# First queries and keys of the prompt's latent attention loaded ahead of stores, and two more page groups of the sample stage fetched within that attention

## The reference

```python
def block(args):                      # mla_prompt, one block of 128 queries
    ql, qr, start = args
    s = (jnp.einsum('bqhc,bkc->bhqk', ql, ckv)
         + jnp.einsum('bqhr,bkr->bhqk', qr, krope)) * MLA_SCALE
    qpos = start + jnp.arange(Q_BLOCK)
    p, _ = masked_softmax_stats(s, kpos[None, :] <= qpos[:, None])
    return jnp.einsum('bhqk,bkc->bqhc', p.astype(ckv.dtype), ckv)
...
ckv_past = cache_ckv[l, page_table].reshape(Bd, past, KV_LORA)
kr_past = cache_krope[l, page_table].reshape(Bd, past, QK_ROPE)
o_lat = mla_sample(ql, qr, ckv, kr, ckv_past, kr_past)
k_cat = jnp.concatenate([cache_win_k[l], kb], axis=1)
```

## Time and profile before

| | before |
|---|---|
| median of three runs | 1953.33 us (1951.91 to 1961.49) |
| profiled execution | 1959.79 us, span 1958.1 us |
| TensorE busy | 1887.9 us, 96% of the span |
| VectorE, ScalarE, GpSimd busy | 1055.5, 887.8, 431.5 us |
| mean granted clock of TensorE | 0.990 |
| DMA | 270.80 MB, mean 138 GB/s |

### The profile page before, as it was taken

One profiled execution on the slowest core, in us unless ns is written; L12 is line 12 of the kernel. 1 busy time (PEld: TensorE's weight loads), 2 busy tenths in 40 slices (PEclk: granted clock), 3 DMA queues, 4 the chain that ended last, 5 costly groups with the idle time before them and its releaser, 6 DMA issues. The chain is left out here.

```text
span 1958.1 us, 47133 instructions
## 1 busy us (share of the span) xinstructions
PE 1887.9 (96%) x18076; PEld 1466.6 (75%) x18076; DVE 1055.5 (54%) x3034; ACT 887.8 (45%) x2042; POOL 431.5 (22%) x569
## 2 busy tenths in 40 slices
PE   7999999999999899999999799999999999999998
PEld 6989898876787667776677466666666688888886
DVE  4433333687854467767677455555556752232232
ACT  5222222688832345566556444344444553333332
POOL 0111111256002130133101322232222411111110
PEclk9999999999999899999999899999999999999999
DMA  8534343743466510112001599777884653333331
GB/s 300 157 108 118 103 122 94 216 124 122 136 167 178 162 55 21 45 44 61 26 18 53 169 297 240 238 217 229 234 247 146 213 194 107 97 97 108 118 101 51
DMA packets 192238, 270.80 MB, mean 138 GB/s; under 512 B 37176, under 2 KB 152328, under 8 KB 183128
## 3 DMA queue, kind: packets, MB, share of 16 engines
q1 hardware_dynamic: 172344, 170.27, 31.0%
q0 software_dynamic: 19712, 98.01, 14.6%
HBM read 212.99 MB, written 54.95 MB: 137 GB/s over the span
## 5 line engine op out<-in xcount | busy, mean ns | idle before, releaser
L102 PE MATMUL proj_acc<-proj_w_hi,proj_x_hi 128*128 128x512 f32 (+2 forms) x512 | 183.9, 359 | 10.2 <-DVE proj_x_lo L372 8.4
L104 PE MATMUL proj_acc<-proj_w_hi,proj_x_lo 128*128 128x512 f32 (+2 forms) x512 | 182.0, 356 | 0.0
L103 PE MATMUL proj_acc<-proj_w_lo,proj_x_hi 128*128 128x512 f32 (+2 forms) x512 | 182.0, 355 | 0.0
L1857 DVE CUSTOM_DVE_ANT_0 mla_probs<-mla_scores,keep_in_rms 128x512 f32<-128x512 f32 x192 | 124.8, 688 | 64.6 <-PE mla_scores L1731 64.2
L1807 ACT ACTIVATE mla_probs<-mla_probs,mla_bias 128x256 f32<-128x256 f32 (+15 forms) x128 | 153.0, 1196 | 12.0 <-DVE mla_bias L1861 7.2
L1731 PE MATMUL mla_scores<-prompt_kr_parts,mla_q_parts 64*128 64x512 f32 (+3 forms) x640 | 136.7, 373 | 0.0
L2208 PE MATMUL dec_scores<-dec_keysT,sample_q_lat 128*64 128x256 f32 x1024 | 124.0, 382 | 3.0 <-DVE dec_keysT L2387 1.8
L2318 ACT ACTIVATE dec_keysT<-dec_turned 128x512 f32<-128x512 f32 (+1 forms) x160 | 89.4, 560 | 65.4 <-PE dec_turned L2164 65.1
L2324 ACT ACTIVATE dec_pT<-dec_outs 128x256 f32<-128x256 f32 x80 | 30.8, 385 | 192.3 <-PE dec_outs L2230 157.8
L102 PEld LDWEIGHTS proj_acc<-proj_w_hi,proj_x_hi 128*128 128x128 f32 x512 | 97.4, 190 | 21.1 <-issue 8.4
L2208 PEld LDWEIGHTS dec_scores<-dec_keysT,sample_q_lat 128*64 128x64 f32 x1024 | 75.4, 138 | 41.2 <-ACT dec_probs L2338 5.0
(11 more groups left out here) (468 smaller groups left out, 4880.2 us busy)
## 6 DMA issues: line engine op xcount, KB each, us to landing
win_v_tile<-wv_out SPq DMA_DIRECT2D x75, 128.0 KB
memory_x_raw<-in_xT SPq DMA_DIRECT2D x17, 512.0 KB, 5.4
proj_rows<-in_x SPq DMA_DIRECT2D x17, 512.0 KB, 4.0
featT<-proj_featT POOLq DMA_DIRECT2D x34, 256.0 KB, 2.8
late_ckv<-in_xT SPq DMA_DIRECT2D x17, 512.0 KB, 6.7
late_ckv<-in_x SPq DMA_DIRECT2D x17, 512.0 KB, 4.3
y_out<-host_buf POOLq DMA_DIRECT2D x16, 512.0 KB, 6.5
dec_k_rows<-in_win_k SPq DMA_DIRECT2D x64, 96.0 KB
```

Source lines behind the costliest of these rows:

```text
L102: pe.matmul(out, lh, rh, start=start, stop=False)
L103: pe.matmul(out, lh, rl, start=False, stop=False)
L104: return pe.matmul(out, ll, rh, start=False, stop=stop)
L1857: dve.tensor_tensor_reduce(probs[:, u % 2, w, c * CH:c * CH + wide], scores[:, n % 3, 0:wide], add, -MLA_SCALE, -LOWEST, ALU.add, ALU.min, ...
```

## The change

Four things are changed.

1. In the latent projections SP issues `first.load` in chunk 2, behind that chunk's key store and the load of chunk 3's input and ahead of the stores of its queries. It stood in chunk 3 behind those stores. The keys of chunk 2 are no longer in it.
2. `first.load_third` stands behind the last key store as before, and now also loads the keys of chunk 2 and the queries of unit 3 (once GpSimd has split unit 1: `q_ready` 2), all ahead of the last stores of queries. `load_q(3)` is gone from the attention's own list.
3. ScalarE's cast of the keys of chunk 2 (`cast_third`) stands ahead of its last product and no longer ahead of five of them.
4. GpSimd fetches three groups of pages (`EARLY`) in the latent attention where it fetched one. Groups 1 and 2 go to `pages_ahead`, in the memory of the even heads' split keys, when the third pair of heads is scored. In the sample stage GpSimd clears the window parts first and then starts from group 3; slots 1 and 2 are empty at first, so that groups 6 and 7 need not wait for a slot. The window rows of sample 1 lie over `pages_ahead`, and their loads also wait for the values of groups 1 and 2.

```diff
-        self.page, self.page_kr = self.buf[:, 0:SEQ], self.buf[:, SEQ:SEQ + self.KR]
-        self.page_loaded, self.page_kr_loaded = b.sem("page_loaded"), b.sem("page_kr_loaded")
+        self.page = self.buf[:, 0:SEQ]
+        self.pages_kr = [self.buf[:, SEQ + l * self.KR:SEQ + (l + 1) * self.KR] for l in range(self.EARLY)]
+        self.pages_loaded, self.pages_kr_loaded = ([b.sem(f"{n}_loaded{l}") for l in range(self.EARLY)] for n in ("page", "page_kr"))
...
-                if c == NCK - 1:
-                    sp.wait_ge(ahead.shares_stored, 16)
-                    sp.wait_ge(new_valued, DEC_B // 2)
-                    sp.wait_ge(k_stored, 16 * c)
-                    sp.wait_ge(qn_stored, 16)
-                    sp.wait_ge(qr_stored, 64)
-                    first.load(sp)
                 sp.wait_ge(act_kept, kept_on_act(c, 7))
                 sp.wait_ge(dve_kept, kept_on_dve(c, 7))
                 sp.dma_start(io["mla_k"].rearrange("(g p) t -> p g t", p=P)[:, :, cols], k_nope[:]).then_inc(k_stored, 16)
                 if c + 1 < NCK:
                     load_cq(c + 1)
-                else:
-                    sp.wait_ge(qn_stored, 16 * c)
-                    sp.wait_ge(qr_stored, 64 * c)
+                if c == NCK - 2:
+                    sp.wait_ge(ahead.shares_stored, 16)
+                    sp.wait_ge(new_valued, DEC_B // 2)
+                    sp.wait_ge(k_stored, 32)
+                    sp.wait_ge(qn_stored, 16)
+                    sp.wait_ge(qr_stored, 64)
+                    first.load(sp)
+                if c == NCK - 1:
+                    sp.wait_ge(qn_stored, 32)
+                    sp.wait_ge(qr_stored, 128)
                     first.load_third(sp)
...
+                        if c == NCK - 1 and i == PER - 2:
+                            first.cast_third(act)
...
-        even_k_hi, even_k_lo = (b.sb(n, [P, SEQ], F32R) for n in ("even_k_hi", "even_k_lo"))
+        with ExitStack() as until_last_heads:
+            even = Buffers(nc, until_last_heads, "mla", owner=owner)
+            even_k_hi, even_k_lo = (even.sb(n, [P, SEQ], F32R) for n in ("even_k_hi", "even_k_lo"))
+        pages_ahead = b.sb("pages_ahead", [P, Host.EARLY - 1, SEQ])
...
-            sp.dma_start(k_raw[:, 2 * CH:3 * CH], io["mla_k"][0:P, 2 * CH:3 * CH]).then_inc(first_k_loaded[2], 16)

         def load_third(sp):
             sp.wait_ge(first_q_ready, 2)
             sp.dma_start(qn_raw[:, 0, :], io["mla_qn"][0:P, 2 * CW:3 * CW]).then_inc(q_loaded[0], 16)
             sp.dma_start(qr_raw[:, 0, :], io["mla_qr"][0:P, 2 * CW:3 * CW]).then_inc(q_loaded[0], 16)
+            sp.wait_ge(prompt.k_stored, 48)
+            sp.dma_start(k_raw[:, 2 * CH:3 * CH], io["mla_k"][0:P, 2 * CH:3 * CH]).then_inc(first_k_loaded[2], 16)
+            sp.wait_ge(q_ready, 2)
+            sp.dma_start(qn_raw[:, 1, :], io["mla_qn"][0:P, 3 * CW:4 * CW]).then_inc(q_loaded[1], 16)
+            sp.dma_start(qr_raw[:, 1, :], io["mla_qr"][0:P, 3 * CW:4 * CW]).then_inc(q_loaded[1], 16)

         def cast_first_k(act, c):
...
-            load_q(3)
...
-            rows = bass.IndirectOffsetOnAxis(ap=sample.rows_of[:, 0:1], axis=0)
+            rows = [bass.IndirectOffsetOnAxis(ap=sample.rows_of[:, l:l + 1], axis=0) for l in range(host.EARLY)]
             pool.wait_ge(k_ready, 4 * (H_A // 2 - 1))
-            pool.indirect_dma_start(host.page, None, ckv_rows, rows).then_inc(host.page_loaded, 16)
+            pool.indirect_dma_start(host.page, None, ckv_rows, rows[0]).then_inc(host.pages_loaded[0], 16)
+            pool.wait_ge(scores_done, 2 * unit_end[NI * (H_A // 2 - 1) - 1])
+            for l in range(1, host.EARLY):
+                pool.indirect_dma_start(pages_ahead[:, l - 1, :], None, ckv_rows, rows[l]).then_inc(host.pages_loaded[l], 16)
             pool.wait_ge(q_ready, 2 * (NU - 1))
-            pool.indirect_dma_start(host.page_kr, None, kr_rows, rows).then_inc(host.page_kr_loaded, 16)
+            for l in range(host.EARLY):
+                pool.indirect_dma_start(host.pages_kr[l], None, kr_rows, rows[l]).then_inc(host.pages_kr_loaded[l], 16)
...
+                if s == 1:
+                    sp.wait_ge(pv_done, past_item[1] + 1)
...
-        for n in range(1, NP):
-            if n == 2:
-                clear_window_parts()
+        clear_window_parts()
+        for n in range(EARLY, NP):
             u = n % AHEAD
-            if 2 <= n < AHEAD:
-                pool.wait_ge(k_turned, 4 * (past_item[n - 2] + 1))
-            if n >= AHEAD:
+            if n >= AHEAD + EARLY:
                 pool.wait_ge(kr_turned, n - AHEAD + 1)
             rows = bass.IndirectOffsetOnAxis(ap=rows_of[:, n:n + 1], axis=0)
             pool.indirect_dma_start(kr[:, u, :], None, kr_rows, rows).then_inc(kr_loaded[u], 16)
-            if n >= AHEAD:
+            if n == AHEAD or n >= AHEAD + EARLY:
                 pool.wait_ge(pv_done, past_item[n - AHEAD] + 1)
             pool.indirect_dma_start(slots[u].rearrange("p m c -> p (m c)"), None, ckv_rows, rows).then_inc(ckv_loaded[u], 16)

...
-                if l:
-                    pe.wait_ge(ckv_loaded[l % AHEAD], 16 * (l // AHEAD + (1 if l % AHEAD else 0)))
-                rows = slots[l % AHEAD]
+                if l >= EARLY:
+                    pe.wait_ge(ckv_loaded[l % AHEAD], loads_of(l))
+                else:
+                    pe.wait_ge(host.pages_loaded[l], 16)
+                rows = page_at(l)
```

48 lines of the change are left out of this document (28 added, 20 removed).

## The result

| | before | after |
|---|---|---|
| median of three runs, us | 1953.33 (1951.91 to 1961.49) | 1935.06 (1932.14 to 1936.93) |
| profiled execution, us (span) | 1959.79 (1958.1) | 1932.14 (1930.4) |
| mean granted clock | 0.990 | 0.995 |

The ratio is 0.9903, 95% interval 0.9877 to 0.9929: 18.3 us less between the medians, forecast 15.8. Two later measurements of the same two kernels gave 0.9916 (0.9896 to 0.9935) and 0.9918 (0.9900 to 0.9937), 16 us.

The account below looks back on a forecast made before the run. TensorE, busy for 96% of the span, was taken as the bound, with time to win at two seams. Latent start -10.5 and sample start -5.3 gave 1953.33 - 15.8 = 1937.5 us; range 1932 to 1947 us.

Parts of the forecast that it names:

- The loads ahead of the stores: Latent start: SP issues the first loads by 634 us, ahead of the query stores; VectorE free at 661.1, not 665.4.
- The 3.46 us stall: Latent start: TensorE's wait for VectorE at the second tile of a score step, to shrink to some 0.5 us.
- the 4.46 us one: Latent start: TensorE's wait ahead of 685.35 for GpSimd's split of unit 3's queries, to vanish with their earlier load.
- The chain of short waits: Latent attention's first score steps: six TensorE pauses of 0.6 us at full clock, 3.6 us; third turn done at 675.6.
- The last store is late next: Latent start: last query store lands at 678.2 and holds VectorE; the step from 689.26 begins at 679.5, 9.8 us earlier.
- Size of the latent half: Latent start: the whole gain there, -10.5 us, with bounds of -5 and -12.5.
- The clock rival: Latent attention's ramp: short pauses make TensorE's clock fall; gain there and at sample start only 13 us, 1940.5 us; chance 0.20.
- two waits of 1.67 and 1.66 us at the sample start that the clock survived: Sample start: argument against the clock falling, since it stood at 1.00 from 1110 to 1115 after such waits.
- The sample start: Sample stage's start: waits of 1.67, 1.66 and 1.96 us for groups 1 to 3 fall, -5.3 us; bounds nothing to -6.
- The rival that the fetch would not cure the wait ahead of group 3's turn: Sample start: that wait names "issue", not a DMA, so only 2 us are won there; 1941 us in all; chance 0.14.
- the copy behind the window mask: Sample start: VectorE's copy for group 1's values ends at 1116.6, and group 3's scores start at 1118.5, not 1123.87.
- The chances: Whole kernel: forecast keeps 0.48; faster 0.76, same 0.16, slower 0.08, with 1943.6 us as the border.

Follow-up runs that it names:

- experiment 5: Changed kernel, but unit 3's queries asked for behind the last query stores, as in the kernel before; ratio to the kernel before 0.9938.
- Experiment 7: Changed kernel with the last chunk's plain query store issued ahead of the four rotary stores; ratio to the kernel before 0.9900.
- experiment 1: Kernel before with only the edits at the latent start, sample stage as before (latent half alone); ratio to the kernel before 0.9950.
- experiment 4: Changed kernel, unchanged, measured and profiled a second time (after again); ratio to the kernel before 0.9916.
- Experiment 6: Changed kernel with only group 1 fetched in the latent attention, group 2 at the sample stage's start ahead of the memsets; ratio to the kernel before 0.9939.
- experiment 8: Changed kernel with the window mask's last step one item later on VectorE (mask split); ratio to the kernel before 0.9910.
- experiment 11: Changed kernel, unchanged, measured and profiled a third time (third profile of after); 1937.59 us, ratio to the kernel before 0.9918.
- experiment 10: Changed kernel with plain query part stored first and the window mask's last step an item later; 1934.17 us, ratio to the kernel before 0.9908.
- before again: Kernel before, unchanged, timed and profiled a second time; ratio 1.000, profiled execution 1953.17 us.
- sample half alone: Kernel before with only the sample-stage edits: groups 1 and 2 fetched during latent attention, memsets first, group 3 into a free slot; ratio 0.9958.
- experiment 9: Kernel before, loading only part of the window rows from the third sample on, so output differs (few window rows); ratio to the kernel before 0.9977.

## Why the prediction held, step by step

**The loads ahead of the stores: right.** SP was through at 634.9 (forecast 634), the first cast stood at 650.58 (649.8), VectorE was free at 661.37 (661.1). The 3.46 us stall became 0.36 (0.5), the 4.46 us one is gone, and experiment 5 brings it back by the one load that was named for it.

**The chain of short waits: right in kind, too long.** Forecast were six pauses of 0.6 us at full clock, 3.6 us. The rows show five, 0.36, 0.36, 0.43, 0.68 and 0.58, 2.4 us. The third turn is done at 675.7 all the same (forecast 675.6), since the last projection ends 0.8 us later here; and the pauses did not set the time of the next step, the store did. The clock is at 1.00 throughout in the profile of after:

```profile
665.00:670.00 5.00, 4.34 (x46) 3.28 (x46) 3.47 (x13) 2.29 (x8) 2.07 (x4) 1.00 0.55 174
670.00:675.00 5.00, 3.74 (x45) 2.67 (x43) 3.51 (x15) 2.94 (x9) 0.00 (x0) 1.00 0.93 260
675.00:680.00 5.00, 3.28 (x43) 2.34 (x41) 2.83 (x10) 2.92 (x7) 0.17 (x1) 1.00 0.38 131
680.00:685.00 5.00, 5.00 (x65) 3.65 (x67) 4.33 (x15) 4.32 (x9) 4.04 (x8) 1.00 0.02 5
```

**The last store is late next: right.** VectorE is held until 678.49 (678.2), the step starts at 679.84 (679.5). Experiment 7 takes just this away.

**Size of the latent half.** Forecast 10.5 us, timed alone 9.8 (5.9 to 13.5), in the first two profiles 10.2 at that step.

**The clock rival was partly true.** After the 1.60 us wait the third profile of after shows this:

```profile
675.00:680.00 5.00, 3.40 (x25) 2.47 (x23) 2.45 (x6) 3.45 (x9) 1.13 (x3) 0.89 0.27 89
680.00:685.00 5.00, 5.00 (x59) 4.18 (x59) 3.91 (x12) 3.35 (x7) 3.06 (x6) 0.77 0.01 2
```

and the mask-split kernel reads 0.80 and 0.86 there. Six profiles have the new latent start and this wait, of 1.60 to 1.75 us (the first and experiments 1, 4, 6, 8 and 11); the clock fell in two of them, and in neither of the two without the wait (experiments 7 and 10). With the fall L is 421.6 and 422.2, without it 419.0 to 420.6. But both of the long ones, and the 420.6 of experiment 4, also had the clock down at the attention's end (0.83, 0.74 and 0.79 from 1075 to 1080, 1.00 in the first profile). Counted only to the value products that begin at 725.59 in the first profile of after, 63.3 us behind the last projection, it is 64.4 and 64.5 with the fall and 63.1 to 63.3 without: the fall costs 1.1 to 1.4 us, and the rival had put it at 2.8. The Trainium skill, page "TensorE: Matmul & The Clock Gate", section "A second HAM failure mode: psum-queue depth-cycling", has the clock swing through such pauses; here the pauses of 0.4 to 0.7 us ahead of it went without a fall in all nine profiles with the new latent start, and the fall came behind the longer wait. What the prediction held against the rival, two waits of 1.67 and 1.66 us at the sample start that the clock survived, was true of that one execution. In the second profile of the same kernel a wait of 1.86 us at the same place was followed by a fall:

```profile
1107.07 1.64 PE L2164 MATMUL dec_turned<-host_ident,late_ckv 64*128 64x64 f32 x32 [1.86 <-DMA late_ckv<-in_cache_ckv,sample_rows_of]
```

```profile
1110.00:1115.00 5.00, 4.86 (x46) 2.75 (x44) 0.71 (x2) 0.38 (x1) 0.95 (x1) 0.56 1.00 291
```

Experiment 1 has the same: a wait of 2.33 us ahead of 1092.59, and a clock of 0.57 from 1095 to 1100. So the clock held in the new ramp in most executions, but not for the reason given.

**The sample start: right in size, partly by luck.** Forecast 5.3, measured 5.6 (26.3 to 20.7 on the mean of three each). The forecast added up three waits of one execution, 1.67, 1.66 and 1.96 us, and put nothing for the clock. TensorE's time between the two marks of S, in the same six profiles:

| profile | idle, us | busy, us | granted clock | S |
|---|---|---|---|---|
| before, first profile | 8.0 | 19.0 | 0.92 | 27.0 |
| before again | 3.8 | 21.8 | 0.77 | 25.6 |
| latent half alone | 5.6 | 20.9 | 0.81 | 26.4 |
| after, first profile | 2.1 | 18.1 | 0.92 | 20.2 |
| after again | 2.1 | 19.1 | 0.87 | 21.1 |
| sample half alone | 2.1 | 18.8 | 0.88 | 20.9 |

On the means the idle time fell by 3.7 us and the busy time by 1.9. The waits were worth less than forecast, and the clock, which fell again at the first of them in two of the three old profiles, gave the rest. The rival that the fetch would not cure the wait ahead of group 3's turn, since that row names "issue", is answered by the other profiles of the old order: there the same wait is 0.59, 1.73 and 1.66 us (before again, experiments 1 and 9) and names the DMA of the rows:

```profile
1121.16 1.21 PE L2164 MATMUL dec_turned<-host_ident,late_ckv 64*128 64x64 f32 x32 [0.59 <-DMA late_ckv<-in_cache_ckv,sample_rows_of]
```

The fetches left at 1061 to 1067, not from 1071, which changes nothing. As worked out there, the copy behind the window mask sets the end: it starts 17.8 us behind the first turn, forecast 19.7 (1116.6 less 1096.92). In the second and third profile of after it is 18.8, with the lower clock of the table of experiment 8, so about 1 us of this difference is the clock. Experiment 6 shows the step to be too generous to one of its parts: one group early is enough for all of S, in one profile.

**The chances** do not add up as written: 0.48, 0.20, and 0.24 less the 0.12 said to be lost make 0.80, not 0.76.

**What the sum left out** is the sample stage behind S, put at nothing. T is 424.3 us on the mean of the three full kernels of the old order and 417.9 of the six of the new order without a wait for window loads. Three things are in it. Of the first profile's 427.0, most of the 7.7 us over the second profile's are the late starts of one execution. Of experiment 1's 426.6, 6.1 are stops without a releaser, the longest of 2.41 us; from there, 1380 to 1385, the granted clock is 0.50. And these stops are shorter in the new order: 3.4, 2.5 and 6.1 us in sum in the three profiles against 0.5 to 1.9 in nine. This last, 1.4 us on the mean of the new ones under the smallest of the old, is the change's own as far as the profiles go, and goes the way from the 5.6 us of S to the 8.2 that were timed. Why it shortens the stops was not tried. The sample half is more than an order of fetches: groups 3 and 4 no longer wait for turns of earlier ones, and the window rows and the mask lie elsewhere in memory; these were not tried apart.

**The 27.7 us between the profiles** are then 12.0 up to the first turn of the sample stage (2.9 of it the first profile of before has over its second, 432.1 and 429.2 for L: 1.1 in the ramp up to the value products named above, and 1.7 at the attention's end, where the granted clock from 1085 to 1095 is 0.77 and 0.84 and held in the second), 6.8 in S, 9.9 in T (mostly the late starts), less 0.9 in the output stage.

## What to carry to other kernels

Where one queue carries stores that wait for computing and loads that wait for nothing, read its order first: here two stalls of 3.5 and 4.5 us at the start of a stage, and a third of 1.7 behind them, were all set by which of them stood ahead. Ask what the next late arrival is before adding up the waits: of 7.9 us of stalls and 4 us of slow clock 10 came back, since a store took over. Before a term is taken from one profile, or a difference of two is explained, profile the same kernel twice: here one execution carried some 7 us of its own in a place that the change hardly touches, and the waits of the sample start were 5.3 us in one execution and some 2.5 in the next, with a lower clock in their place.

## What had not been expected of the hardware

**TensorE stops that follow the DMA load, and end with a packet of instructions.** In the sample stage TensorE stops in the middle of a row of equal matmuls, with no releaser, at the same instructions in each execution: near 26, 103 and 267 us behind S in the old order, 0.3 to 2.4 us each, and in three profiles also between 315 and 323 us (0.3 to 0.9). The third of them in the changed kernel and in the sample half alone:

```profile
1369.15 0.44 PE L2242 MATMUL dec_scores<-dec_krT,sample_q_rot 64*64 64x128 f32 x6 [0.51 <-issue]
```

```profile
1377.94 0.44 PE L2235 MATMUL dec_scores<-dec_krT,sample_q_rot 64*64 64x128 f32 x6 [1.60 <-issue]
```

With fewer bytes in flight the second and third are gone (experiment 9). Beside the data the trace has two queues that load instructions, here over the whole of the kernel before:

```profile
q8 instruction: 126, 2.06, 0.4%
q14 instruction: 56, 0.46, 0.1%
```

The packed traces hold the start and length of each packet of q8, 126 of 16,384 bytes. The thirteen profiles have 24 stops at these five places, and each ends 1.26 to 1.62 us behind the end of a packet, at one place always of the same packet of the queue. (One stop more, of 0.22 us in the first profile of before, lies at no such place.) The places lie 1123, 2371, 624 and 126 matmuls apart and their packets 9, 19, 5 and 1: some 125 matmuls with as many weight loads for each. The third place in six profiles:

| profile | matmul starts behind the packet's end, us | stop, us |
|---|---|---|
| before, first profile | 1.35 | 1.36 |
| before again | 1.46 | 1.60 |
| latent half alone | 1.43 | 2.41 |
| after, first profile | 1.31 | 0.51 |
| after again | 1.38 | 1.05 |
| few window rows | 8.12 | none |

In none of the 65 cases does the matmul start sooner than 1.26 us behind its packet. So the stops are waits for TensorE's own instructions, as closely as these traces can show it. That the packet comes late because the data stand ahead of it fits experiment 9, and was not shown directly. The Trainium skill, page "Runtime: NRT & Kernel Launch", section "Instruction fetch mechanics", says that an engine's instructions come by its own DMA queue in blocks, and calls the cost mostly hidden. The traces agree with the blocks (16,384 bytes each), and with the cost in most cases: of the some 50 packets between S and the end of T one to five are waited for, up to 2.4 us each.

**VectorE late for a whole stage, once.** Reads of scores started some 0.4 us late in 41 of 63 cases, in one execution of thirteen profiled, and with them came seven waits of 0.35 to 0.40 us on TensorE ahead of the scores of the window's rest.
